# Gate halves of small experts added on VectorE, expert rows stored plainly and fetched twice

## The reference

```python
def moe_swiglu(h, w_router, w1, w3, w2):
    logits = (h @ w_router).astype(jnp.float32)
    top_val, top_idx = lax.top_k(logits, TOP_K)                  # 2 of 8 experts
    top_w = jax.nn.softmax(top_val, axis=-1)
    combine = jnp.sum(jax.nn.one_hot(top_idx, N_EXPERTS, dtype=jnp.float32) * top_w[..., None], axis=-2)
    out = jnp.zeros_like(h)
    for e in range(N_EXPERTS):
        out = out + combine[..., e:e + 1].astype(h.dtype) * swiglu(h, w1[e], w3[e], w2[e])
    return out

def reference(x, mem, ...):
    for layer in range(DEPTH):                                   # DEPTH = 2
        h = rms_norm(x, norm_mix_g[layer])
        x = x + hybrid_mixer(h, ...)                             # three causal mixers, gated
        x = x + memory_cross_attention(rms_norm(x, norm_x_g[layer]), ...)
        h = rms_norm(x, norm_ffn_g[layer])
        x = x + (swiglu(h, ...) if layer % 2 == 0 else moe_swiglu(h, ...))
    return rms_norm(x, final_g)
```

## Time and profile before

| what | value |
|---|---|
| median of 3 runs | 1801.12 us |
| profiled execution | 1802.62 us |
| its span, first to last instruction | 1800.9 us |
| TensorE busy (matmuls) | 1778.0 us, 99% |
| VectorE busy | 1507.2 us, 84% |
| ScalarE busy | 1207.6 us, 67% |
| GpSimd busy | 85.8 us, 5% |
| DMA, queue 1 (weights) | 507.83 MB, 70.7% of 16 engines |
| DMA, queue 0 (GpSimd's) | 9.18 MB, 1.7% |
| granted clock of TensorE | 0.997 of full speed |

### The profile page before, as it was taken

The page is one execution under the profiler, slowest core; times in us unless marked ns, Lnnn a source line. Parts: engine busy times, 40 slices in busy tenths (PEclk is TensorE's granted clock), DMA queues, the critical chain, the costliest instruction groups (busy, mean ns, idle before and its releaser), DMA issues.

```text
span 1800.9 us, 24793 instructions
## 1 busy us (share of the span) xinstructions
PE 1778.0 (99%) x10058; PEld 1525.1 (85%) x10058; DVE 1507.2 (84%) x1402; ACT 1207.6 (67%) x1135; POOL 85.8 (5%) x97
## 2 busy tenths in 40 slices
PE   9999999999999999999999999999999999999997
PEld 9989898899999989898888887877878777787775
DVE  7999866566557999876579898999989899998997
ACT  5657754454445557654576787878878787787785
POOL 1000000100001000000100001001010010000000
PEclk9999999999999999999999999999999999999999
DMA  8444555345554544454468999999999999999995
GB/s 342 180 172 142 186 187 187 118 164 210 186 182 158 193 177 141 169 223 169 154 229 315 417 427 407 426 427 420 427 402 428 425 423 421 406 426 425 416 415 222
DMA packets 55826, 519.87 MB, mean 289 GB/s; under 512 B 7136, under 2 KB 7392, under 8 KB 12320
## 3 DMA queue, kind: packets, MB, share of 16 engines
q1 hardware_dynamic: 52448, 507.83, 70.7%
q0 software_dynamic: 2544, 9.18, 1.7%
q10 hardware_dynamic: 720, 1.31, 0.2%
HBM read 511.74 MB, written 6.55 MB: 288 GB/s over the span
## 4 chain that ended last, share of the span: by engine, by line
PE 84%; DVE 10%; ACT 4%; issue 2%; DMA 1%; SPq 0%; ACTq 0%; DVEq 0%
PE psum L2140 15%; PE psum L2126 13%; PE psum L2128 13%; PE psum L2127 13%; PE psum L2141 8%; PE psum L2634 7%; PE psum L2635 7%; DVE raw_alias L1374 3%; DVE U_alias L1374 2%; DVE wlo L1374 2%; ACT whi L832 1%; PE psum L2647 1%; PE psum L2629 1%; PE psum L2653 1%; ACT wlo L832 1%
## 5 line engine op out<-in xcount | busy, mean ns | idle before, releaser
L832 ACT ACTIVATE whi<-raw 128x2048 fp32r<-128x2048 f32 (+1 forms) x225 | 424.0, 1896 | 68.9 <-PE psum L2141 50.0
L1374 DVE TENSOR_TENSOR wlo<-raw,whi 128x2048 fp32r<-128x2048 f32 (+1 forms) x144 | 326.3, 2267 | 131.6 <-ACT whi L832 131.3
L2140 PE MATMUL psum<-h_hl,whi 128*128 128x512 f32 x1216 | 430.6, 398 | 0.3 <-DVE U L1732 0.2
L2141 PE MATMUL psum<-h_hl,wlo 128*128 128x256 f32 x1216 | 340.4, 280 | 0.0
L2140 PEld LDWEIGHTS psum<-h_hl,whi 128*128 128x128 f32 x1216 | 228.2, 188 | 55.4 <-issue 1.2
L2141 PEld LDWEIGHTS psum<-h_hl,wlo 128*128 128x128 f32 x1216 | 229.5, 189 | 0.1
L1374 DVE TENSOR_TENSOR raw_alias<-raw,wlo 128x2048 fp32r<-128x2048 f32 x87 | 196.5, 2284 | 18.4 <-ACT wlo L832 18.2
L2126 PE MATMUL psum<-act_hl,whi 128*128 128x256 f32 x720 | 206.1, 286 | 0.9 <-DVE wlo L1374 0.5
L2127 PE MATMUL psum<-act_hl,whi 128*128 128x256 f32 x720 | 203.7, 283 | 0.0
L2128 PE MATMUL psum<-act_hl,wlo 128*128 128x256 f32 x720 | 203.6, 283 | 0.0
L1374 DVE TENSOR_TENSOR raw_alias<-raw,whi 128x2048 fp32r<-128x2048 f32 x81 | 183.4, 2285 | 13.6 <-ACT whi L832 13.5
(11 more groups left out here) (335 smaller groups left out, 3379.4 us busy)
## 6 DMA issues: line engine op xcount, KB each, us to landing
raw<-in_stream SPq DMA_DIRECT2D x87, 2048.0 KB, 15.5
raw<-in_stream SPq DMA_DIRECT2D x141, 1024.0 KB, 4.8
U<-in_stream SPq DMA_DIRECT2D x52, 2048.0 KB, 14.2
memhat<-in_stream SPq DMA_DIRECT2D x29, 1024.0 KB, 11.1
h_hl_alias<-in_stream SPq DMA_DIRECT2D x29, 1024.0 KB, 13.1
raw<-in_stream SPq DMA_DIRECT2D x6, 512.0 KB, 3.7
xacc<-U POOLq DMA_DIRECT2D x3, 512.0 KB, 8.0
xT<-in_x_cols ACTq DMA_DIRECT2D x4, 256.0 KB, 6.9
```

Source lines behind the costliest of these rows:

```text
L832: act.activation(hi_home(n)[:, first:words], src[:, first:words], ACT.Copy).then_inc(hi_ready, 1)
L1374: dve.tensor_tensor(lo_home(n)[:, first:words], src[:, first:words], hi_home(n)[:, first:words].bitcast(F32), ALU.subtract).then_inc(lo_re ...
L2140: pe.matmul(o[:].rearrange("p (a b) -> p a b", a=2), st[0], mv, start=start, stop=False)
L2141: return pe.matmul(o[:, 0:256], st[1], mv[:, 0, :], start=False, stop=stop)
```

## The change

1. *Gate halves.* The fold matmul of the gate goes. ScalarE copies only the bank's upper 64 partitions to the lower 64 of `gsum`, VectorE adds the bank's lower half (`gate_summed`), and ScalarE takes Silu of the sum twice, once into each half of `esil`, one chunk earlier than before (`silu_end`).
2. *Rows stored plainly.* `ys` has a row of zeros and 128 rows for each of places 0 to 6. The scatter writes rows there without addition. `yidx` lists for each token where its two rows are (`rows_listed`, VectorE, 8 small instructions at chunk 16): the later place in columns 0 and 1, the earlier in 2 and 3; 0 is the row of zeros.
3. *Empty slots skipped.* Their indices lie out of bounds, in the gathers and in the scatters, and the DMA leaves them out.
4. *Fetched twice.* The earlier rows are fetched by two indirect DMAs to `xa` before place 6's scatter, the later ones by two more to `xsum` after it.
5. *Additions late.* x is no longer written to HBM. Its first 128 tokens are turned by TensorE at step 53 and added by VectorE (`kept_added`, chunks 325 and 326), the others are added in the final banks by 8 matmuls. Four additions of `xsum` stand at chunks 329 to 332 of 0 to 335 (`halves_added`). `final_rows` waits for them.
6. *Clearing.* ScalarE issues seven DMAs of 512 KB that write a constant to `ys` during layer 1's mixer (chunks 30 to 36 of the layer).

```diff
+FAR, CLEARED = 2048, 30
...
-def folded_end(s):
-
-    return up_end(s) + 1 if s < STEPS - 1 else up_end(s)
+def silu_end(s):
+
+    return up_end(s) if s < STEPS - 1 else gate_end(s) + 1
+
+
+def hidden_end(s):
+
+    return silu_end(s) + 1 if few_step(s) else up_end(s)
...
+        xsum = act_plain[:, 2048:4096].rearrange("p (b d) -> p b d", b=TB)
...
-        xacc = nc.dram_tensor("xacc", [S + SLOTS, D], F32).ap()
+        ys = nc.dram_tensor("ys", [1 + (NE - 1) * SLOTS, D], F32).ap()
...
             gp.wait_ge(hr_in, 16)
-
-            def kept(t):
-
-                gp.wait_ge(xt_ready, 2 * t + 2)
-                gp.dma_start(xacc[P * t:P * t + P, :], xtok).then_inc(scr_in, 16)
-
-            kept(0)
             gp.wait_ge(ix_ready, 1)
...
                 gp.indirect_dma_start(out=hg[0:there, :], out_offset=None, in_=hrow,
-                                      in_offset=bass.IndirectOffsetOnAxis(ap=gidx[0:there, p:p + 1], axis=0))\
-                  .then_inc(hg_in, 16)
+                                      in_offset=bass.IndirectOffsetOnAxis(ap=gidx[0:there, p:p + 1], axis=0),
+                                      bounds_check=S - 1, oob_is_err=False).then_inc(hg_in, 16)
+
+            def sums_in(to, first):
+
+                for b in range(TB):
+                    at = first + b
+                    gp.indirect_dma_start(out=to[:, b, :], out_offset=None, in_=ys,
+                                          in_offset=bass.IndirectOffsetOnAxis(ap=yidx[:, at:at + 1], axis=0)).then_inc(xa_in, 16)
...
                 if e == 0:
                     rows_in(1)
-                    kept(1)
-                    gp.dma_start(xacc[S:S + SLOTS, :], xtok).then_inc(scr_in, 16)
                     rows_in(2)
-                    gp.wait_ge(scr_in, 48)
+                    gp.wait_ge(scr_in, 16 * NE)
+                if e == NE - 2:
+                    gp.wait_ge(ga_done, NE)
+                    sums_in(xa, TB)
                 if e < NE - 1:
                     here = HALF if few(e) else SLOTS
                     gp.wait_ge(y_ev, e + 2)
-                    gp.indirect_dma_start(out=xacc, out_offset=bass.IndirectOffsetOnAxis(ap=sidx[0:here, e:e + 1], axis=0),
-                                          in_=y[0:here, :], in_offset=None, compute_op=ALU.add).then_inc(y_sent, 16)
+                    gp.indirect_dma_start(out=ys, out_offset=bass.IndirectOffsetOnAxis(ap=sidx[0:here, e:e + 1], axis=0),
+                                          in_=y[0:here, :], in_offset=None,
+                                          bounds_check=(NE - 1) * SLOTS, oob_is_err=False).then_inc(y_sent, 16)
...
-            gp.wait_ge(ga_done, NE)
-            gp.dma_start(xa, xacc[0:S, :].rearrange("(b p) d -> p b d", p=P)).then_inc(xa_in, 16)
+            sums_in(xsum, 0)
...
+                    p = n - BASE[1] - CLEARED
+                    if 0 <= p < NE - 1:
+                        act.dma_start(ys[1 + SLOTS * p:1 + SLOTS * p + SLOTS, :].rearrange("p (a b) -> p a b", a=DB),
+                                      ones[:].unsqueeze(1).to_broadcast([P, DB, P])).then_inc(scr_in, 16)
...
                         if few_step(s):
-                            act.activation(gsum, bank[gate_bank(s)][:], ACT.Copy).then_inc(halves_out, 1)
+                            act.activation(gsum[0:HALF, :], bank[gate_bank(s)][HALF:P, :], ACT.Copy).then_inc(halves_out, 1)
...
-                    s = due(n, folded_end)
+                    s = due(n, silu_end)
                     if s is not None and few_step(s):
-                        act.wait_ge(folded, folds(s) + 1)
+                        act.wait_ge(gate_sum, folds(s) + 1)
                         act.wait_ge(e_g, s - 1)
-                        act.activation(esil[:, s % 2, :], bank[gate_bank(s)][:], ACT.Silu).then_inc(e_silu, 1)
+                        act.activation(esil[0:HALF, s % 2, :], gsum[0:HALF, :], ACT.Silu)
+                        act.activation(esil[HALF:P, s % 2, :], gsum[0:HALF, :], ACT.Silu).then_inc(e_silu, 1)
...
+            def kept_added(i):
+
+                t, at = i // 2, slice(512 * (i % 2), 512 * (i % 2) + 512)
+                if i == 0:
+                    dve.wait_ge(xa_in, 16 * TB)
+                dve.wait_ge(xt_done, i + 1)
+                dve.tensor_tensor(xa[:, t, at], bank[4 + i][:], xa[:, t, at], ALU.add).then_inc(xt_ready, 1)
+
+            def halves_added(i):
+
+                t, at = i // 2, slice(512 * (i % 2), 512 * (i % 2) + 512)
+                dve.wait_ge(xa_in, 32 * TB)
+                dve.wait_ge(xt_ready, 2)
+                dve.tensor_tensor(xa[:, t, at], xsum[:, t, at], xa[:, t, at], ALU.add).then_inc(xa_sum, 1)
...
+            def gate_summed(s):
+
+                dve.wait_ge(halves_out, folds(s) + 1)
+                dve.tensor_tensor(gsum[0:HALF, :], bank[gate_bank(s)][0:HALF, :], gsum[0:HALF, :], ALU.add).then_inc(gate_sum, 1)
...
+                    if s is not None and few_step(s):
+                        gate_summed(s)
...
+                    if n in (325, 326):
+                        kept_added(n - 325)
+                    if n in (329, 330, 331, 332):
+                        halves_added((2, 3, 0, 1)[n - 329])
...
-            def folded_gate(s):
-
-                pe.wait_ge(halves_out, folds(s) + 1)
-                pe.matmul(bank[gate_bank(s)][:], fold, gsum, start=True, stop=True).then_inc(folded, 1)
...
                     at = 512 * (i % 2)
+                    pe.wait_ge(xa_sum, (2, 3, 0, 1).index(i) + 1)
                     pe.matmul(final_bank(0, i // 2, i % 2), ident[:], xa[:, i // 2, at:at + 512],
                               start=True, stop=False, skip_group_check=True)
+                    if i > 1:
+                        for k in range(4):
+                            c = 4 * (i % 2) + k
+                            pe.matmul(final_bank(0, 1, i % 2)[:, P * k:P * k + P], xT[:, c, P:S], ident[:],
+                                      start=False, stop=False, skip_group_check=True)
...
+                    if s == STEPS - 3:
+                        pe.wait_ge(y_ev, NE)
+                        for i in range(TB):
+                            xrows(i)
```

101 lines of the change are left out of this document (51 added, 50 removed).

## The result

The change makes the kernel slower: 1811.76 us (median of 6 runs, 1807.70 to 1815.09) against 1801.46 (6 runs of before, 1800.34 to 1802.88). The ratio is 1.0053, 95% interval 1.0042 to 1.0063. The forecast was 1790, its range 1781 to 1799. The profiled execution has a span of 1806.7 us.

What follows compares the result with a forecast made beforehand. TensorE and the DMA were taken as both at their limit, with the DMA's non-weight traffic to be won: 0 - 4 - 10.5 + 3 = -11.5 us from the profiled 1802.6, medians 1.5 lower, so 1790; range 1781 to 1799.

Steps and rivals of the forecast that it cites:

- the last fetch: Near the end: two fetches side by side land at 1763 to 1767, before VectorE's addition at 1768.0 needs them; counted 0.
- Rival D: Near the end: the last fetches, served one after the other, land 13 us late and stall VectorE; 1803 to 1808, chance 0.09.
- Fold matmuls out, 0: Second layer's expert stage: 24.1 us less on TensorE, counted 0 because the DMA holds step pairs at 29.4 to 29.5 us.
- at their limit: Second layer's expert stage: TensorE and the DMA both full, within a few tenths of a us.
- Gate halves on VectorE, 0 in the body: Expert stage: 28 additions of 0.60 us, 16.8 us, paid for in the body by VectorE's 42.2 us of idle time.
- Rows, -10.5: Expert stage: fewer and plainly stored rows save DMA time for weights, 10.5 us, bounds 5 to 11.5.
- The body in sum: Expert stage before its end: a gain of 10.5 us, all from the rows' DMA saving.
- Rival A: Expert stage: VectorE becomes the bound, only 3 to 7 us of gain are left, 1794 to 1798; chance 0.16.
- Start, -4: Start of the expert stage: no write of x to HBM and four groups of transposes fewer save 4 us, between 1.8 and 5.7.
- Clears, 0: Seven clearing writes between about 728 and 766 us fit into free DMA time; counted 0, bound +5.
- The end, +3 within 0 to 5.4: Behind 1737 us: nine more additions, 5.4 us, on a VectorE without gaps, part absorbed; +3 us.
- its 22 additions in the body: VectorE check of the body: 42.2 us idle less 16.2 for 22 additions, time shrinking by 10.5, leaves some 15 us.

Runs made afterwards that it cites:

- e3: Changed kernel without its last two fetches and the wait for them; the late additions add x's columns instead, later rows missing from the output: 1801.35 us, ratio 0.9998.
- e14: Changed kernel in which VectorE starts the splits of chunks 314 to 326 only when its split before is complete: 1801.80 us, ratio 1.0002.
- e6: Separate kernel, no weights loaded: GpSimd fetches 128 rows and copies a column, twice in each of six VectorE patterns; fetches took 0.96 to 77.76 us.
- e9: Kernel before with the fold matmul out and no addition of the gate halves at all (lower halves missing from the output): 1803.81 us, ratio 1.0007.
- e1: Kernel before with the first edit alone, fold matmul out and gate halves added by VectorE: 1801.13 us, ratio 0.9994.
- e10: Kernel before with gate halves added by VectorE up to step 50 and by TensorE's fold matmul from step 51 on: 1802.30 us, ratio 0.9996.
- e2: Changed kernel with the gate's fold matmul on TensorE and ScalarE's whole copy as in before, so the rows edit alone: 1804.42 us, ratio 1.0012.
- e7: Changed kernel without the last two fetches, the wait for them and VectorE's gate additions (output incomplete): 1795.44 us, ratio 0.9971.
- e11: Changed kernel with the gate's fold matmul back on TensorE from step 51 on: 1800.85 us, ratio 0.9991.

## Why the prediction was wrong

The step that failed is **the last fetch, "it just makes it; I count 0"**. It costs 10.4 us (after less e3), the lower clock behind the stall included. The forecast took 13.7 us from issue to landing and the two fetches side by side, to land between 1763 and 1767; the trace gives 17.5 and 18.3 us, of which 7.88 and 11.16 on GpSimd, one behind the other, with 5.57 more for the copy ahead, and 1770.56. With GpSimd let in (e14) they are 13.8 and 16.7 us and 1763.40: the DMA's part was priced right, the issue on GpSimd was not. The rows that it used gave no warning: before's five gathers of that stretch took 1.4 to 2.8 us on GpSimd, although VectorE stood still for at most 0.03 us beside any of them. That an instruction on GpSimd can take another price beside other VectorE work was nowhere in the sum, although it noted for VectorE "almost no gap" at the end and put nine more instructions there. The Trainium skill (SBUF — State Buffer, "Who interferes with whom") has the rule that was missed: VectorE and GpSimd share a port pair as "an exclusive lock", and a VectorE instruction with two SBUF inputs contends with a GpSimd instruction that reads SBUF. The trace agrees, and goes further: 75.42 us in e6, over some 34 instructions, not one.

The fetch is not the only failed step. Without the wait (e3) the kernel takes 1801.35 us, still above the forecast's 1799: start, body and end together brought next to nothing of the 11.5 us gain that they were to add up to.

Rival D had the place right, VectorE's queue at the addition, but another mechanism (fetches served one after the other at 16.1 us) and a chance of 0.09 with the price added to a gain of 11.5 us that didn't come either.

The other terms, by the table:

- *Fold matmuls out, 0.* Worth 5.0 us in the body (e9), 3.3 and 4.1 with the additions (e1, e10). TensorE was the tighter of the two "at their limit": the DMA's relief alone gave 0.0 (e2).
- *Gate halves on VectorE, 0 in the body.* Cost 5.4 us (e7 against e3). The 42.2 us of waits did not pay for all: 27.3 stayed.
- *Rows, -10.5.* The price per row was right (10.5 ns against 10), queue 0's time too (14.2 us against 12.9). Saved time of the queue is not saved time of the kernel: 8.2 us less in 1034:1779 gave 5.0 in the body (e7 against e9), and nothing with TensorE in the way (e2).
- *The body in sum*: -10.5 forecast, -4.6 measured over 604 of the 745 us. Rival A, VectorE becomes the bound, had 3 to 7 us of gain, and e7 shows its mechanism at work.
- *Start, -4.* Where the profiled execution has the same two falls of the clock as before's (0.91 in 905:925 and in 965:985) it is -0.8 (e7) and, with the rows alone, +0.3 (e2). The -3.9 of the changed kernel's own trace is luck: its clock did not fall there. What makes it fall is open; TensorE was busy 20.00 of 20 us in 965:985 in both.
- *Clears, 0.* Right: TensorE 10.00 of 10, and 41.92 of 42 over their whole stretch.
- *The end, +3 within 0 to 5.4.* 5.6 without the wait (e3), counted from the 50th split on. VectorE has 12 additions more there, about 7.2 us at 0.60, so little was absorbed.

With the start at -0.8: -0.8 - 4.6 + 5.6 = +0.2, so 1801.7 against e3's 1801.35. One slip of the forecast changes nothing: its 22 additions in the body are 13.2 us at 0.60, not 16.2.

## What to carry to other kernels

A price read for an instruction of GpSimd, an indirect DMA's issue too, holds only beside the same VectorE work: where an engine is filled to the last gap, price again what shares something with it. A pause of 0.1 us between instructions that are always ready can be worth 10 us. And where three resources are all nearly full (here 99%, 94% and all of the DMA), relief of one is worth what the next allows; size it by leaving the other's work out, not by adding up what is saved. Last, set runs at the same granted clock side by side before a few us are put down to an edit.

## What the runs showed of the hardware

A GpSimd fetch of 128 rows by index takes 0.96 us on the engine with VectorE idle, 2.8 us beside gapless two-input subtractions in the free case and 75 us, all of their time, in the held case. 128x2048 copies at 1.22 us held it for 77.76 us. In the two kernels of phases, of one execution each, a stretch of two-input splits alone was free when it began after a standstill of VectorE and held when it began while VectorE ran on, and a pause of 0.1 us undid the hold; why is open. The real kernels do not follow that rule by their pauses alone: e11 was free and the changed kernel held, both some 9 us behind a pause. A row of 4 KB cost all 16 DMA engines 20.5 ns when it was added to HBM and 10.5 ns when it was stored plainly. After 8.78 us without work TensorE ran at half clock, a matmul every 0.43 us instead of 0.23.
